# Wide attention stage, norms before the Fourier stage, fp32 rows 64 bytes off, and another spread of the modulation chunks

## The reference, cut to what matters

```
for l in range(2):
    mx = split(silu(c) @ w_mod[l] + b_mod[l], 9)      # 9216 columns
    ...
    x = x + 0.5 * mx[2] * swiglu(modulate(rms_norm(x), mx[0], mx[1]), ...)
    hx = modulate(rms_norm(x), mx[3], mx[4]) @ w_in[l]
    mix_x, mix_z = token_mixing(hx, hz, ...)
    x = x + mx[5] * (mix_x @ w_out[l])
    x = x + 0.5 * mx[8] * swiglu(modulate(rms_norm(x), mx[6], mx[7]), ...)
...
token_mixing: a = real(fft2(fourier part))
              b = neighborhood attention (4 heads, bias, own and context keys)
              c = gated linear attention, q and k decayed by log_sigmoid gates
              d = grouped-query attention (4 heads over 2), own and context keys
              concatenate a, b, c, d
```

## Time and profile before

| | |
|---|---|
| median of 3 runs | 3516.27 us (3513.65 to 3518.14) |
| profiled execution | 3517.91 us |
| its span, first to last instruction | 3515.8 us |
| mean granted TensorE clock | 0.945 |
| PE busy | 3237.6 us, 92 % |
| PE weight loads busy | 2949.5 us, 84 % |
| DVE busy | 1922.0 us, 55 % |
| ACT busy | 1641.8 us, 47 % |
| POOL busy | 152.6 us, 4 % |
| HBM read | 552 MB, 157 GB/s |

### The profile page before, as it was taken

The page is one execution under the profiler, slowest core; times in us unless marked ns, Lnnn a source line. Parts: engine busy times, 40 slices in busy tenths (PEclk is TensorE's granted clock), DMA queues, the critical chain, the costliest instruction groups (busy, mean ns, idle before and its releaser), DMA issues. The chain is left out here.

```text
span 3515.8 us, 54378 instructions
## 1 busy us (share of the span) xinstructions
PE 3237.6 (92%) x23014; PEld 2949.5 (84%) x23014; DVE 1922.0 (55%) x2904; ACT 1641.8 (47%) x2444; POOL 152.6 (4%) x143
## 2 busy tenths in 40 slices
PE   6999899998999999999898778999999999999898
PEld 4899788897779998899798557999989898989797
DVE  5455465555546655555545325445575656566655
ACT  5444455544445444444444314435654444665343
POOL 0000000001000000000100100000110101101100
PEclk8999999998999999999999758999999999999899
DMA  6665344553435555765355303546435554434464
GB/s 217 204 217 178 130 144 156 192 180 113 124 123 189 168 184 180 235 204 167 110 162 171 114 12 117 183 144 194 126 109 191 168 186 156 147 116 134 155 196 138
DMA packets 464997, 556.67 MB, mean 158 GB/s; under 512 B 25285, under 2 KB 431733, under 8 KB 464373
## 3 DMA queue, kind: packets, MB, share of 16 engines
q1 hardware_dynamic: 464756, 553.20, 48.6%
HBM read 552.12 MB, written 1.05 MB: 157 GB/s over the span
## 5 line engine op out<-in xcount | busy, mean ns | idle before, releaser
L259 DVE TENSOR_TENSOR wl<-wr,wh 128x1024 fp32r<-128x1024 f32 x702 | 826.7, 1213 | 238.2 <-ACT wh L251 236.6
L251 ACT ACTIVATE wh<-wr 128x1024 fp32r<-128x1024 f32 x702 | 700.5, 1039 | 154.4 <-DMA wr<-in_ffn_w_dram 105.7
L116 PE MATMUL psum<-xt_hi,wh 128*128 128x256 f32 (+1 forms) x2000 | 576.9, 288 | 9.8 <-DVE xt_lo L2539 5.0
L117 PE MATMUL psum<-xt_lo,wh 128*128 128x256 f32 (+1 forms) x2000 | 569.5, 285 | 0.0
L118 PE MATMUL psum<-xt_hi,wl 128*128 128x256 f32 (+1 forms) x2000 | 569.5, 285 | 0.0
L1833 DVE TENSOR_TENSOR wl<-wr,wh 128x1024 fp32r<-128x1024 f32 (+3 forms) x336 | 388.9, 1197 | 94.0 <-ACT wh L1825 92.6
L116 PEld LDWEIGHTS psum<-xt_hi,wh 128*128 128x128 f32 (+1 forms) x2000 | 386.0, 193 | 18.7 <-issue 6.3
L117 PEld LDWEIGHTS psum<-xt_lo,wh 128*128 128x128 f32 (+1 forms) x2000 | 386.3, 193 | 2.2
L118 PEld LDWEIGHTS psum<-xt_hi,wl 128*128 128x128 f32 (+1 forms) x2000 | 385.9, 193 | 0.1
L116 PE MATMUL psum<-wh,xt_hi 128*128 128x256 f32 (+1 forms) x1280 | 376.9, 294 | 3.0 <-ACT vv L2945 1.5
L1825 ACT ACTIVATE wh<-wr 128x1024 fp32r<-128x1024 f32 (+3 forms) x336 | 322.7, 997 | 108.8 <-DMA wr<-in_mlp_w_dram 74.5
(11 more groups left out here) (444 smaller groups left out, 5716.9 us busy)
## 6 DMA issues: line engine op xcount, KB each, us to landing
wr<-in_ffn_w_dram SPq DMA_DIRECT2D x231, 1024.0 KB, 5.1
wr<-in_w_in_dram SPq DMA_DIRECT2D x88, 1024.0 KB, 5.1
wr<-in_w_mod_dram SPq DMA_DIRECT2D x72, 1024.0 KB, 4.9
wr<-in_mlp_w_dram SPq DMA_DIRECT2D x64, 1024.0 KB, 5.1
wr<-in_w_out_dram SPq DMA_DIRECT2D x20, 1024.0 KB, 5.0
wr<-in_mem_w_kv_dram SPq DMA_DIRECT2D x8, 1024.0 KB, 4.8
wr<-in_w_branch_dram SPq DMA_DIRECT2D x16, 512.0 KB, 3.5
wr<-in_w_branch_dram SPq DMA_DIRECT2D x8, 1024.0 KB, 4.8
```

The costliest lines, as they stand in the source:

```text
L116: pe.matmul(out, a[0], b[0], start=first, stop=False)
L117: pe.matmul(out, a[0], b[1], start=False, stop=False)
L251: act.activation(self.high[s][:, r], self.raw[s][:, r], ACT.Copy).then_inc(self.highs.sem, 1)
L259: dve.tensor_tensor(self.low[s][:, r], self.raw[s][:, r], self.high[s][:, r].bitcast(F32), ALU.subtract).then_inc(self.lows.sem, 1)
```

## The change

1. For X of layer 1 the attention is the new class `WideAttention`. It uses psum banks 0 to 5 (two each for scores, transposes and outs), two buffers each for the masked scores and `probs_t`, and 8 columns instead of 4 for the small head buffers. A step issues the scores of unit u, the transposes of unit u-2 and the outs of unit u-3; there are n+3 steps instead of 3(n+1). As the banks 0 to 3 belong to the turnings else, the attention now also waits for `z_t9`, and the squares of X (`sq_x3`) wait for the end of the mixer's turn.
2. In three mixers `norms()` comes before `spectral()` in the background list.
3. The weight ring moves down by 128 bytes. `xt`, `zt`, `dqk`, `ot_diff`, `mem_t`, `mem_t2`, `merged` and `latents_t` move down by 64 bytes, `ot_mem` up by 64 bytes. `gated`, `square`, `ot_mla` and the other buffers stay. This holds in both parts.
4. Of the last modulation pieces, 2 instead of 3 stand at the turning `z_t9`, 8 instead of 5 at the state and attention (with 6 steps each), 2 instead of 4 at the turning `x_t9`.

```diff
+RING_SHIFT, ROW_SHIFT = 1 / 8, 1 / 16
...
-        self.raw = [self.at(f"wr{s}", [P, CHUNK], F32, 16 * s) for s in range(RING)]
-        self.low = [self.at(f"wl{s}", [P, CHUNK], F32R, 16 * s) for s in range(RING)]
-        self.high = [self.at(f"wh{s}", [P, CHUNK], F32R, 16 * s + 8) for s in range(RING)]
+        self.raw = [self.at(f"wr{s}", [P, CHUNK], F32, 16 * s - RING_SHIFT) for s in range(RING)]
+        self.low = [self.at(f"wl{s}", [P, CHUNK], F32R, 16 * s - RING_SHIFT) for s in range(RING)]
+        self.high = [self.at(f"wh{s}", [P, CHUNK], F32R, 16 * s + 8 - RING_SHIFT) for s in range(RING)]
...
-    xt = pair("xt", KT, 64, 8)
-    dqk = at("dqk", [P, 2, 2048], F32, 80)
-    otd = pair("ot_diff", KT, 80, 8)
+    xt = pair("xt", KT, 64 - ROW_SHIFT, 8)
+    dqk = at("dqk", [P, 2, 2048], F32, 80 - ROW_SHIFT)
+    otd = pair("ot_diff", KT, 80 - ROW_SHIFT, 8)
...
-    xt = [pair("xt", 80), pair("zt", 64)]
+    xt = [pair("xt", 80 - ROW_SHIFT), pair("zt", 64 - ROW_SHIFT)]
...
+class WideAttention(HeadAttention):
+    def __init__(self, w, units, buf, before, mask=None):
+        super().__init__(w, units, buf, before, mask)
+        self.n_steps = self.n + 3
+    def pe(self, pe):
...
+        for u in range(n + 3):
+            if u < n:
+                if u >= 2:
+                    pe.wait_ge(self.probs.sem, self.probs.at(u - 1))
...
+                    o = w.ps[:, u % 2, i * 256:(i + 1) * 256]
...
+            a = u - 2
+            if 0 <= a < n:
+                pe.wait_ge(self.probs.sem, self.probs.at(a + 1))
+                if a >= 2:
+                    pe.wait_ge(self.moved.sem, self.moved.at(a - 1))
...
+                    last = pe.transpose(w.ps[:, 2 + a % 2, i * P:(i + 1) * P], buf["p"][:, a % 2, i * P:(i + 1) * P], w.eye)
...
+            a = u - 3
+            if 0 <= a < n:
+                pe.wait_ge(self.moved.sem, self.moved.at(a + 1))
+                if a >= 2:
+                    pe.wait_ge(self.done.sem, self.done.at(a - 1))
...
+                    last = pe.matmul(w.ps[:, 4 + a % 2, 0:HD], buf["pt"][:, a % 2, i * P:(i + 1) * P], un["v"][i], start=(i == 0),
...
...
-    background += [After(w, x_in1.last)] + xm1.spectral() + xm1.norms() + xm1.decays(x_in1.gt) + xm1.head_turns()
+    background += [After(w, x_in1.last)] + xm1.norms() + xm1.spectral() + xm1.decays(x_in1.gt) + xm1.head_turns()
...
-    order += M1[24:27]
+    order += M1[24:26]
...
-    background += xm1.attention(bias1, zk.na_turn.wait_done, zk.g_turn.wait_done)
-    for p_ in M1[27:32]:
+    background += xm1.attention(bias1, zk.na_turn.wait_done, zk.g_turn.wait_done, z_t9.wait_done)
+    for p_ in M1[26:34]:
         p_.steps = 6
-    order += M1[27:32]
+    order += M1[26:34]
...
-    sq_x3 = Squares(w, waits(x_out1.wait_added, z_t9.wait_done), X.x, X.ss)
+    sq_x3 = Squares(w, waits(x_out1.wait_added, xm1.turn.wait_done), X.x, X.ss)
...
-    order += M1[32:36]
+    order += M1[34:36]
```

More of the change, by code:

```diff
@@ L3258, in first_block @@
              for kind, n in (("na", 8), ("gqa", 6), ("gla", 4))}
-    att = {k: small(f"head_{k}", 4) for k in ("neg", "sums", "inv")}
+    att = {k: small(f"head_{k}", 8) for k in ("neg", "sums", "inv")}
     assert small_kb[0] <= 185
@@ L3332, in __init__ @@
             self.na_t = own(s, l, "na_t", [P, 4, TOK], 8)
-            self.buf = dict(att, p=own(s, l, "probs", [P, 2, 512], 0), sm=own(s, l, "masked", [P, 512], 4), pt=own(s, l, "probs_t", [P, 512], 6))
+            self.wide = l == 1
+            self.buf = dict(att, p=own(s, l, "probs", [P, 2, 512], 0))
+            if self.wide:
+                self.buf.update(sm=own(s, l, "masked", [P, 2, 512], 4), pt=own(s, l, "probs_t", [P, 2, 512], 12))
+            else:
+                self.buf.update(sm=own(s, l, "masked", [P, 512], 4), pt=own(s, l, "probs_t", [P, 512], 6))
             for k in att:
@@ L3410, in attention @@
             first = waits(self.na_turn.wait_done, self.out.wait_done, self.gla_norm_squares, self.proj.wait_done, *ready)
-            self.na = HeadAttention(w, units, self.buf, first if z else waits(first, bias_in.wait), None if z else self.mask)
+            kind = WideAttention if self.wide else HeadAttention
+            self.na = kind(w, units, self.buf, first if z else waits(first, bias_in.wait), None if z else self.mask)
             units = []
@@ L3422, in attention @@
                     units.append(u)
-            self.gqa = HeadAttention(w, units, self.buf, waits(self.g_turn.wait_done, self.na.wait_done))
+            self.gqa = kind(w, units, self.buf, waits(self.g_turn.wait_done, self.na.wait_done))
             self.turn = MixTurn(w, mix, s.pair, waits(self.gqa.wait_done, self.gla_norm.wait_done, self.fourier.wait_done), lambda eng: None)
@@ L3468, in first_block @@
     zf1.pieces[4].fetch += [zm.gla_in.fetch, layer_in[0].fetch, rope_in.fetch]
-    background += [After(w, z_in.last)] + zm.spectral() + zm.norms() + zm.decays(z_in.gt) + zm.gla_out()
+    background += [After(w, z_in.last)] + zm.norms() + zm.spectral() + zm.decays(z_in.gt) + zm.gla_out()
     zm.st = GlaState(w, zm.cols("gla_k", P), zm.cols("gla_v", 256), a, zm.dec, zm.se, zm.kd, state, waits(zm.out.wait_done, z_in.wait_done))
@@ L3498, in first_block @@
     body[0].fetch += [xm.dft_in.fetch, xm.gla_in.fetch]
-    background += [After(w, x_in.last)] + xm.spectral() + xm.norms() + xm.decays(x_in.gt)
+    background += [After(w, x_in.last)] + xm.norms() + xm.spectral() + xm.decays(x_in.gt)
     background += xm.gla_out(zm.st.wait_done, dqi=xm.dqi, state=state) + xm.head_turns()
```

83 lines of the change are left out of this document (75 added, 8 removed).

## The result

The changed kernel takes 3381.05 us (median of 4 runs, 3376.61 to 3390.11) against 3517.2 us before; the ratio is 0.9617, with a 95% interval of 0.9595 to 0.9638. That is 136 us less, where 98 were forecast.

The account below looks back on a forecast made before the run. PE is busy 3237.6 of 3515.8 us; beyond 278 us idle, gains need pace or clock. Terms 34 + 50 + 5 + 7, and 2 for the out-projection, make 98 off 3517.9; adjusted to the median, 3418, range 3328 to 3448.

Parts of the forecast that it names:

- the likeliest case: Whole kernel: norms, attention and turnings gain, offsets give zero; 3418 us, own range 3395 to 3445, chance 0.51 with D.
- Rival A: Dense matmuls: part of 6.5 ns is a clash of weight and moving reads at like addresses; 3333 to 3375, chance 0.32.
- Offsets: Ring and row buffers moved: taken as zero, bounds 85 us won and 85 us lost over 13,056 matmuls.
- Norms: Norms before the Fourier stage at three places: 11, 13 and 10 us won, sum 34, bounds 17 and 44.
- The table's wait: PE's wait before `dft_tok` for the Fourier table's load: of 7 us some 1.3 stay, under 2 at all places.
- The gate's wait: PE's wait before `gate_w` for a memset on DVE, 6.18 us at place 3: goes but for 1 us.
- the copies and one split: DVE work still ahead of the gate's memset after the norms move: put at 1 us of remaining wait.
- Attention: Last attention, wide: clock rises within its first units and stays, 133 us become 81; 50 us won after a bias load.
- Rival B: Last attention stays at the slow level since modulation chunks bring waits for DVE's splits: 9 instead of 50, 3459; chance 0.12.
- Turnings: `z_t9` and `x_t9` with fewer modulation chunks lose waits for DVE's splits: 5 and 7 us won, bounds 0 and 15.
- C: Dense matmuls: the same offsets lengthen the pace, 0.1333 instead of 0.120 loses 174 us, 3592; chance 0.05.
- D: Norms go first, yet DVE is late for the splits: 17 instead of 34, 3435; chance within the forecast's 0.51.

## Why the prediction was right or wrong

**The time lay in the range, but below the likeliest case's own.** That case, 3395 to 3445, had the offsets at nothing, and 37 us separate its value from the measured one. The first rival, A, gave 3333 to 3375 and a chance of 0.32; it is what happened, a little above its upper end. The case's own range doesn't follow from its terms: 29 us more and 28 less than 3418 are 3447 and 3390, not 3445 and 3395. And 3328 lies below the whole of A, though it was to leave the outermost part of A out.

**Offsets.** The step that failed: I took zero, since 0.120 against 0.1137 follows the width of the stationary operand with the addresses unchanged. Both are true. The width is one way to the faster pace and the address difference another, and the first said nothing against the second. The rule of the Trainium skill beside it ("TensorE: Matmul & The Clock Gate", on the weight load: two independent read ports) led the same way and does not hold as far as pace goes: with TensorE alone the same instruction takes 0.113 to 0.120 by where the operands lie. Rival A was right in kind and in order: 3.3 ns times 13,056 were forecast for its upper time, 2.8 and 4.6 were measured. It left out that the 512-column form could lose, 12.3 us.

**Norms.** Forecast 34, bounds 17 and 44; 27.5 by the stretches, 30 by the run with nothing else. The table's wait went as described at all three places: 2.1, 2.0 and 1.5 us are left of some 7 each, where under 2 was forecast. The gate's wait went whole at place 1, but stayed at 4.2 at place 2 and 2.4 at place 3, not the 1 us I gave it. The mis-sized term is "the copies and one split": I had counted DVE's work, not that DVE at place 3 waits 3.57 us for the Fourier matmuls in front of that memset. The Trainium skill's rule on DVE beside GpSimd ("SBUF — State Buffer", "Who interferes with whom") is borne out by a row: 2.99 us for two halves, against 2.4 without company.

**Attention.** Forecast 81 us for the stretch, measured 79.8. The number was right and the reason wrong, so the number is luck: I had the clock rise within the first units because PE has no gap. It rose 27 us after the first score, inside a chunk, and the fast units after it were as short as forecast. The run without chunks shows 89.2 us, and 0.50 from about 2008 us on to its end, nearly without gaps. The window that I leaned on, 1980.5 to 1987.7, stands right behind a chunk in which the clock rose, and at which I didn't look:

```profile
1977.73 2.05 PE L651 MATMUL psum<-wh,silu 128*4 128x256 f32 x8
1979.62 1.09 PE L651 MATMUL psum<-wl,silu 128*4 128x256 f32 x8
```

So it shows matmuls that keep the fast level for 7 us, not that they bring it. Rival B had the stage stay slow, at a chance of 0.12, since chunks would bring gaps. In these traces it is with the chunks that the clock rises. The wide stage with two chunks inside is 16.7 us shorter in the traces than the one with none (72.5 against 89.2), though it does more; the first is the fastest of its four executions and the second the slowest, and by the medians the kernels are 21 us apart, of which some 9 are the longer last turning. The price for the stage at the slow level, 124 us, was too high as well: without chunks it measured 89.2, and five chunks of 3.9 on top make 109.

**Turnings.** Forecast 5 and 7, measured 3.7 and 7.7. The chunk's split went from the chain; at `z_t9` the diagonal matmuls ran partly at the slow level (6.67 us instead of 4.24), and from their start to the next piece it took 9.5 us, where the forecast had fixed 8.4. At `x_t9` the sum of 16.7 came out near (15.8) by luck: 8.3 ahead of the diagonal matmuls and 8.4 behind were forecast, 10.3 and 5.5 measured.

**The prediction's rivals C and D.** No form of 256 columns got slower, so C fell; the 512-column one did get slower. D (norms first only moves DVE's lateness) fell too: the `wl` waits of the first part's ordinary pieces are 14.8 us in all against 14.1.

## What stays open

That chunks bring the fast level rests on one trace without them and eight with them; a stage without chunks wasn't repeated. Why the clock fell again in the second half of the wide stage with the old spread and didn't in the run of the wide stage alone, which has the same order there, is not settled; nor is which property of a chunk's matmuls brings the fast level (their type, their 128 rows, or both), since no run changed one alone. What the reads share that gives a period of 256 bytes can't be seen from here, nor why a run of matmuls keeps the pace that it starts with; nor was it tried whether the good pace can be forced in the kernel, say by a few matmuls at another difference ahead of a piece. An estimate from the table: 3.5 ns x 9216 + 1.5 x 3840 = 38 us for these two groups.

## What to carry to other kernels

In a kernel that is bound by short matmuls, measure the start-to-start time of each form and shift one operand's buffer by 64 bytes against the other's before anything else. The change is one constant, and each form has its own best place. A stage in which TensorE is busy for all of its time can still run at the slow level: look at the granted clock of its window, and try whether other work of TensorE, put into it, lifts it. And what a wide stage gains can hang on the other work that stands in it (55 us with two chunks inside, 37 with none, some 9 of the difference being the longer last turning), so test such changes apart and together.

## What was not expected of the hardware

- Matmuls of 256 columns against 128 start every 120.0 ns with the operands' addresses equal modulo 256 bytes, 118.6 at 128 bytes apart, and 117.8 or 113.3 at 64 or 192; of 512 columns every 227 ns at 0, 233 at 64, 232 or 233 at 128, 229 at 192. Of the two addresses only the difference counts, and no other engine has to run.
- At 64 and 192 two paces exist for the same instructions, and the group ahead decides which.
- In the run without chunks TensorE stayed at 1.2 GHz for 74 us in which it was idle for 0.7 us.
